# Weight tiles in SBUF: 32 bytes of gap behind each k tile, and a start 112 bytes past a multiple of 128

## The reference

```
x = LN(a*x + 0.5 * (silu(x @ w_gate) * (x @ w_up)) @ w_down)      # FFN1
z = x @ w_in    # -> q, k, v | conv b, c, h | two gates
y_attn = rmsnorm(differential attention(q, k, v)) @ w_attn_out    # prompt; sample over 1024 cached tokens
y_conv = (b * short_conv(c * h)) @ w_conv_out
x = LN(a*x + (sigmoid(g_attn)*y_attn + sigmoid(g_conv)*y_conv) @ w_o)
x = LN(a*x + 0.5 * swiglu(x; FFN2 weights))
```

## Time and profile before

| | |
|---|---|
| median of 3 runs | 2282.65 us (2281.95 to 2284.63) |
| profiled execution, span from first to last instruction | 2280.6 us, 2.05 us below the median |
| TensorE busy | 2265.8 us, 99% |
| weight loads busy (overlap the matmuls) | 2234.5 us, 98% |
| VectorE busy | 1366.8 us, 60% |
| ScalarE busy | 996.6 us, 44% |
| matmuls | 18574 |

### The profile page before, as it was taken

How to read it: one execution, slowest core, us unless ns; L and a number is a source line. 1 busy time by engine, 2 the same in 40 slices (tenths; PEclk the granted TensorE clock), 3 DMA queues, 4 the chain that set the end, 5 groups by cost and what they waited for, 6 DMA issues and landing times.

```text
span 2280.6 us, 45670 instructions
## 1 busy us (share of the span) xinstructions
PE 2265.8 (99%) x18574; PEld 2234.5 (98%) x18574; DVE 1366.8 (60%) x1523; ACT 996.6 (44%) x1236; POOL 29.7 (1%) x59
## 2 busy tenths in 40 slices
PE   9999999999999999999999999999999999999997
PEld 9999999999999999999998899999999999999997
DVE  5444454444655689999975457886444544445554
ACT  5344444443434454454543454554343434433333
POOL 1000000000000001000000000000000000000001
PEclk9999999999999999999999999999999999999999
DMA  7555555555555588989988855555555555555553
GB/s 247 191 175 184 179 178 182 172 186 180 178 183 177 192 277 287 322 287 325 330 303 315 294 171 192 180 175 184 184 172 187 172 186 175 184 179 180 178 182 115
DMA packets 233440, 475.47 MB, mean 208 GB/s; under 512 B 18449, under 2 KB 21889, under 8 KB 233313
## 3 DMA queue, kind: packets, MB, share of 16 engines
q1 hardware_dynamic: 225920, 465.22, 61.6%
q0 software_dynamic: 2320, 5.68, 0.8%
q10 hardware_dynamic: 5072, 2.78, 0.4%
HBM read 468.13 MB, written 4.43 MB: 207 GB/s over the span
## 4 chain that ended last, share of the span: by engine, by line
PE 95%; DVE 4%; DMA 0%; issue 0%; POOL 0%; ACT 0%; SPq 0%; DVEq 0%; ACTq 0%
PE ps L638 30%; PE ps L639 30%; PE ps L640 29%; PE ps L750 1%; PE ps L752 1%; PE ps L751 1%; DVE w_lo L1368 1%; PE ps L893 1%; DVE kv_ring L1701 1%; DVE scores L1707 1%; DMA kv_ring<-in_cache_v 0%; POOL y L621 0%; PE ps L781 0%; DMA w_raw<-in_ffn_w_gate 0%; PE ps L857 0%
## 5 line engine op out<-in xcount | busy, mean ns | idle before, releaser
L1368 DVE TENSOR_TENSOR w_lo<-w_raw,w_hi 128x1024 fp32r<-128x1024 f32 x750 | 912.7, 1223 | 806.2 <-ACT w_hi L990 803.6
L990 ACT ACTIVATE w_hi<-w_raw 128x1024 fp32r<-128x1024 f32 x750 | 789.4, 1058 | 1033.0 <-PE ps L640 995.3
L638 PE MATMUL ps<-x_hi,w_hi 128*128 128x264 f32 x3840 | 1095.2, 285 | 0.4 <-DVE w_lo L1428 0.4
L639 PE MATMUL ps<-x_lo,w_hi 128*128 128x264 f32 x3840 | 1091.5, 284 | 0.0
L640 PE MATMUL ps<-x_hi,w_lo 128*128 128x264 f32 x3840 | 1091.2, 284 | 0.0
L638 PEld LDWEIGHTS ps<-x_hi,w_hi 128*128 128x128 f32 x3840 | 724.0, 189 | 12.7 <-issue 7.4
L639 PEld LDWEIGHTS ps<-x_lo,w_hi 128*128 128x128 f32 x3840 | 722.8, 188 | 0.0
L640 PEld LDWEIGHTS ps<-x_hi,w_lo 128*128 128x128 f32 x3840 | 721.3, 188 | 0.0
L638 PE MATMUL ps<-h_hi,w_hi 128*128 128x264 f32 x1408 | 401.1, 285 | 0.0
L639 PE MATMUL ps<-h_lo,w_hi 128*128 128x264 f32 x1408 | 400.5, 284 | 0.0
L640 PE MATMUL ps<-h_hi,w_lo 128*128 128x264 f32 x1408 | 400.2, 284 | 0.0
(11 more groups left out here) (268 smaller groups left out, 1369.8 us busy)
## 6 DMA issues: line engine op xcount, KB each, us to landing
w_raw<-in_ffn_w_down SPq DMA_DIRECT2D x176, 512.0 KB, 3.7
w_raw<-in_ffn_w_gate SPq DMA_DIRECT2D x175, 512.0 KB, 3.5
w_raw<-in_ffn_w_up SPq DMA_DIRECT2D x175, 512.0 KB, 4.3
w_raw<-in_w_in SPq DMA_DIRECT2D x160, 512.0 KB, 4.9
kv_ring<-in_cache_k SPq DMA_DIRECT2D x64, 512.0 KB, 6.1
kv_ring<-in_cache_v SPq DMA_DIRECT2D x64, 512.0 KB, 6.3
w_raw<-in_w_o SPq DMA_DIRECT2D x32, 512.0 KB, 4.2
w_raw<-in_w_conv_out SPq DMA_DIRECT2D x16, 512.0 KB, 5.6
```

What stands on the lines that cost most here:

```text
L638: nc.tensor.matmul(acc, wh, hi[:, kt], start=(kt == 0), stop=False)
L639: nc.tensor.matmul(acc, wh, lo[:, kt], start=False, stop=False)
L990: nc.scalar.activation(w_hi[:, s], w_raw[:, s], ACT.Copy).then_inc(w_hi_ready, 1)
L1368: V.tensor_tensor(w_lo[:, s], w_raw[:, s], w_hi[:, s].bitcast(F32), ALU.subtract).then_inc(w_lo_ready, 1)
```

## The change

The split rings w_hi and w_lo get 8 float32 (32 bytes) behind each k tile of 512 columns, so that k tiles are 2080 bytes apart and slots 4160. The ring begins at an address 96 past a multiple of 128, and its first tile 16 bytes further on, 112 past; w_lo lies 16640 bytes, again a multiple of 128, behind w_hi. w_raw, where the DMA writes, stays as it is. To make room, pick goes behind hid into the area, neg_eye, s_tmp and o_sqs go into the region of the layer norm's tensors, and neg_eye is written by VectorE just before its use instead of at the start. The area is now rounded to a multiple of 128; it stays at 110720, and x, h, raw, yc, o and m keep their addresses.

```diff
@@ -59,6 +59,7 @@
 HEAD_STATS = 22
 LATE = DT - MC
 RAW = N + 2
+LINE, W_GAP, W_FIRST = 128, 8, 4
 
 
 class Count:
@@ -136,8 +137,19 @@
         y = at("y", [P, DT, N], F32, x_at)
         y_norm = at("y_norm", [P, DT, N], F32, x_at + DT * TILE)
         w_raw = at("w_raw", [P, RING, KC, WC])
-        w_hi = at("w_hi", [P, RING, KC, WC], F32R)
-        w_lo = at("w_lo", [P, RING, KC, WC], F32R)
+        lam_in = at("lam_in", [HD, 4])
+        lam_prod = at("lam_prod", [HD, 2])
+        lam = at("lam", [P, 4])
+        SPLIT_RING = RING * KC * (WC + W_GAP)
+        w_at = -(-(top + 32) // LINE) * LINE - 32
+
+        def spaced(flat):
+
+            return flat[:, W_FIRST:W_FIRST + SPLIT_RING].rearrange("p (s k n) -> p s k n", s=RING, k=KC)[:, :, :, 0:WC]
+
+        w_hi = spaced(at("w_hi", [P, W_FIRST + SPLIT_RING], F32R, w_at))
+        w_lo = spaced(at("w_lo", [P, W_FIRST + SPLIT_RING], F32R, w_at + SPLIT_RING * 4))
+        top = w_at + (W_FIRST + 2 * SPLIT_RING - W_GAP) * 4
         ident = at("ident", [P, P])
         ones = at("ones", [P, P])
         mask = at("mask", [P, 3, P])
@@ -147,13 +159,8 @@
         conv_state = at("conv_state", [P, AT, B, 2])
         rope_cs = at("rope_cs", [ROWS, 2, ROT])
         subln = at("subln", [P, 1])
-        lam_in = at("lam_in", [HD, 4])
-        lam_prod = at("lam_prod", [HD, 2])
-        lam = at("lam", [P, 4])
         page_ids = at("page_ids", [1, 2, B * PAGES], I32)
-        pick = at("pick", [P, GROUPS, HEADS, SEQS])
         group_rows = at("group_rows", [P, GROUPS])
-        neg_eye = at("neg_eye", [ROWS, ROWS])
         ln_at = (top + 31) // 32 * 32
         one_sum = at("one_sum", [P, N])
         sq_sum = at("sq_sum", [P, N])
@@ -166,12 +173,13 @@
         eps = at("eps", [P, 2])
         warm = at("warm", [P, 1])
         first_wg = at("first_wg", [P, 2, MC, 2])
-        area = (top + 31) // 32 * 32
+        area = -(-top // LINE) * LINE
 
 
         h_hi = at("h_hi", [P, FT, N], F32R, area)
         h_lo = at("h_lo", [P, FT, N], F32R, area + FT * TILE)
         hid = at("hid", [P, MC, N], F32, area + 2 * FT * TILE)
+        pick = at("pick", [P, GROUPS, HEADS, SEQS], F32, area + (2 * FT + MC) * TILE)
         raw = at("raw", [P, 2 * DT, RAW], F32R, (area + 2 * FT * TILE - 2 * MC * RAW * 4) // 32 * 32)
         mean_rstd = mean_sq
         first_gu = at("first_gu", [P, 2, MC, N], F32, area + (2 * FT - 5 * MC) * TILE)
@@ -242,8 +250,6 @@
         o_lo = at("o_lo", [P, AT, N], F32R, c_at + 2 * AT * TILE)
 
         stats = at("stats", [P, HEADS, HEAD_STATS])
-        s_tmp = at("s_tmp", [ROWS, 2])
-        o_sqs = at("o_sqs", [P, HEADS * B])
 
         u = z_c[:, 2]
         conv_o = z_c[:, 1]
@@ -258,6 +264,10 @@
         s_rec = at("s_rec", [P, SEQS * 2 * HEADS], F32, ln_at + 5120)
         s_diag = at("s_diag", [SEQS * 2 * HEADS, SEQS * 2 * HEADS], F32, ln_at + 5376)
         s_col = at("s_col", [SEQS * 2 * HEADS, 1], F32, ln_at + 5632)
+        s_tmp = at("s_tmp", [ROWS, 2], F32, ln_at + 5664)
+        o_sqs = at("o_sqs", [P, HEADS * B], F32, ln_at + 5696)
+        neg_eye = at("neg_eye", [ROWS, ROWS], F32, ln_at + 5952)
+        assert ln_at + 5952 + ROWS * 4 <= mean_at + 3 * TILE
 
         def s_attn(g):
 
@@ -1455,7 +1465,6 @@
                 for g in range(GROUPS):
                     V.tensor_reduce(group_rows[:, g:g + 1], pick[:, g].rearrange("p h s -> p (h s)"), AX, ALU.add
                                     ).then_inc(rows_ready, 1)
-                V.tensor_scalar(neg_eye[:], ident[0:ROWS, 0:ROWS], -NEG, NEG, ALU.mult, ALU.add)
                 then(V.tensor_scalar(subln[:], subln[:], 1.0 - LAMBDA_INIT, None, ALU.mult))
 
             def split_with_x():
@@ -1785,6 +1794,7 @@
                     v.wait_ge(s_roped, 2)
                     then(V.tensor_tensor(q_s[:], q_s[:], qk_s[:], ALU.mult))
                 if part == 1:
+                    V.tensor_scalar(neg_eye[:], ident[0:ROWS, 0:ROWS], -NEG, NEG, ALU.mult, ALU.add)
                     V.memset(scores[:, :, PAGES], NEG)
                     then(V.tensor_reduce(s_tmp[:], q_s[:].rearrange("p (g d) -> p g d", d=HD), AX, ALU.add))
                 if part == 2:
```

## The result

The change takes 2279.98 us (median of 20 runs, 2278.99 to 2281.24) against 2282.89 us before (20 runs, 2281.87 to 2284.82). The ratio is 0.9987, 95% interval 0.9981 to 0.9993: 2.9 us, 0.13%, a small gain that lies within what I had called no change. I had forecast 2262, with 0.61 on faster by over 0.2%. The time lies inside my range, but of the 20 us of gain that I had forecast only 2.9 came. Two of all the executions, one of before (4486.61 us) and one of the kernel with only the small tensors moved (8777.42 us), were in a slow state and count in no ratio.

The account below looks back on a forecast made before the run. The prediction took TensorE's step from matmul to matmul as the bound, not waiting. A gain of 20.3 us over x, m and yc, all else priced 0, gave 2262 us from a span of 2280.6; range 2246 to 2294.

Parts of the forecast that it names:

- no change: Whole kernel: a time within 0.2%, 4.6 us, of the time before.
- (a): Over x, m and yc, 12,672 matmuls: constant distance between weight and moving addresses makes every step 0.120 us, gaining 20.3 us.
- the 0.13 steps: Two of 12 steps from 201.52 to 202.98 us, both first product of the odd k tile; the other ten took 0.120.
- Rival 2: Over x, m and yc the constant distance is a poor one: 11.4 us more, 2294 us; chance 0.12.
- (a) over h: 4,608 matmuls over h and o: no gain taken, since hi and lo keep two distances; upper end 9.7 us.
- The sum: Whole kernel: span 2280.6 - 20.3 = 2260.3 us, median 2.05 us above it, so 2262.4, said as 2262.
- the tight stretch: 850 to 1180 us, where VectorE is busy 313.0 of 330 us, 17 us free.
- (b): Weight tiles starting 16 bytes past a multiple of 32: price taken as nothing, upper bound 27.6 us over 17,280 matmuls.
- (c): Writes of w_hi and w_lo as two rows of 512 with a gap: price 0, 10 us if each grew 0.2.
- (d): Moved small tensors and constants, and neg_eye written later on VectorE: price 0, or 0.2 us if uncovered.
- Rival 4: VectorE binds between 850 and 1180 us through the split writes: 10 us back, 2272 us; chance 0.05.
- Rival 1: TensorE's matmuls: distance between weight and moving addresses doesn't matter, steps stay as before, 2282.65 us; chance 0.12.

Follow-up runs that it names:

- D = 96: The change with weight minus moving tile address, modulo 256, constant at 96 instead of 112: 2291.54 us, ratio 1.0039.
- D = 32: The change with weight minus moving tile address, modulo 256, constant at 32 instead of 112: 2273.10 us, ratio 0.9956; with k outside m as well, 2269.74 us.
- D = 64: Group in a kernel of matmuls alone, weight minus moving tile address 64 modulo 256, both addresses still: 0.120 us a step.
- D = 160: Group in a kernel of matmuls alone, weight minus moving tile address 160 modulo 256, both addresses still: 0.126 us a step.
- D = 128: The change with weight minus moving tile address, modulo 256, constant at 128 instead of 112: 2285.38 us, ratio 1.0013; with k outside m as well, 2268.02 us.
- D = 0: Weight minus moving tile address 0 modulo 256: still groups of matmuls alone, 0.1200 us a step at 264 columns; the change with it, 2277.16 us.

## Why the prediction was wrong, point by point

*What bounds the kernel* was right: TensorE's step, not waiting, at a full clock, and something beyond the 110 ns of columns in it. The changed kernels moved as their steps over x and h did.

*(a), the constant distance, is the step that failed.* It was "if the distance is constant, all steps are as the other ten, 0.120". I took the 0.13 steps for the place where the price is paid, and the ten others for the state without it. That was a reading of half a chunk: over whole panels of before, the steps outside the slow place have 0.1213 on average and all steps 0.1217, from the starts, so even without that place only 12,672 x (0.1217 - 0.1213) = 5 us were there to gain. The timeline after shows constant distance and the same spread of 0.11 to 0.13, in another pattern. What changes from tile to tile isn't only the distance: with distance kept, the place of both addresses modulo 256 still moves by 32 bytes at each k tile. The step over x went to 0.1211, so 12,672 x 0.0005 = 6.3 us could come of the 20.3, if all of these matmuls gained it. That distances differ was right and is shown by D = 96 and D = 32; that a constant one is as good as the quick steps isn't: of five constant distances with k inside, three are better over x than before (0, 32, 112), one is worse (96) and one is both (128). Rival 2, a poor distance, is what 96 is; 112 is in the middle.

*(a) over h* I had at no gain, with 9.7 us as the other end. It was a loss: 4,608 x 0.0003 = 1.4 us. I had seen that hi and lo keep two distances there, and priced it from one side only. I had also not seen that the distance of the hi products changes by 128 from panel to panel there.

*The sum*, term by term, of the profiled executions: the two long stretches over x, 7,680 matmuls, give 3.9 us by the counts; the other 4,992 over x, m and yc, most of them between attention's own matmuls, give 0.7 by their starts; h costs 1.4; the tight stretch stands still 1.1 us longer. That is 2.1, and the spans differ by 1.2; the counts are good to one matmul in 3848, and the two panels side by side cost 0.2. The medians differ by 2.9 us, since the profiled execution of after was 1.3 us above its own, which is about the idle time that it shows.

*(b), the odd start*, at nothing: right, as far as the start without gaps shows it. Raw's higher step, from which I took its upper bound, isn't that price: still groups of raw's 266 columns, with weight tiles at multiples of 32, have 0.1222 against 0.1200 with 264.

*(c) and (d)*: w_hi takes 1059 ns and w_lo 1223, as before to 1 ns, and the moved tensors alone measure as nothing. Right.

*Rival 4*, VectorE in the middle, is out: in the tight stretch TensorE waited for no w_lo, and the two quickest kernels, at 2269.74 and 2268.02 us, stood still there for 1.1 and 0.9 us.

*Rival 1* gave 2282.65, nearly the result, for a wrong reason: distances do matter, they only gain little at 112.

*The rule on two independent read ports* (the Trainium skill, "TensorE: Matmul & The Clock Gate", Part 2), by which loading the next weights takes nothing from the running matmul: this case doesn't agree with it. With the moving tile still and only the weight tile's address another, D = 64 has 0.120 and D = 160 has 0.126 us a step at the same clock and tile sizes. Yet a load of 32 columns leaves the step where a load of 128 has it. The case doesn't tell how the two reads meet.

What stays open: the mechanism. That the places of both addresses set the steps, but for patterns with two of them, is shown; why a place costs what it does, and what picks one of two steps for one pattern, isn't. Steps that wait for turns of a fixed rhythm would fit the two steps at D = 128, but not the uneven ones over the widths; no run took it apart.

## What to carry to other kernels

A difference between steps in a timeline says where a rhythm shows, not what it would be without its cause: before pricing a pattern from its quick members, measure the pattern that the edit makes. Here that is cheap, since a kernel that only issues the matmuls with the kernel's addresses modulo 256 gave nearly all steps over x to 0.0001 us, for dozens of layouts in one run. It must hold every phase that the kernel has (here the panels that begin at slot 2) and issue each block more than once, since one pattern can have two steps. Try place and loop order together: neither the gap (2285) nor the order (2282) gains at D = 128, both together give 2268.02 us, 0.9934 of the time before and the best of all that was run.

## What the runs showed of the hardware

- Matmuls of 264 columns don't start at even steps though nothing holds them up: 0.116 to 0.130 us, in a pattern that repeats with the addresses. With both addresses still the step is 0.120 at D = 64 and 0.126 at D = 160, and at D = 96 it is 0.1217 or 0.1200 by where the pair lies.
- Tiles 1280 bytes apart, which all start at one place modulo 256, have 0.1200 over x at D = 0 and 64 and 0.1233 at D = 128, where tiles 1056 apart have 0.1217 without the gap.
- Weight loads of 32 columns take 109 ns and of 128 columns 189, and the step of 264 moving columns is 0.120 with either.
- The step doesn't rise evenly with the columns: 0.1187 at 260, 0.1222 at 262, 0.1200 at 264, 0.1267 at 270, 0.1253 at 272, both addresses still at D = 0.
- One sequence of instructions over one set of addresses ran at two paces in one execution: 3796 and 3839 matmuls in 466 us at D = 128.
